# First mixer pair prepared among the last projection units of a fused two-block kernel

## The chip, the cores and the metric

The kernel runs on one core of a Trainium2 chip. The metric is the device time of one execution in microseconds, lower is better. Three runs of the kernel before gave 3347.84, 3348.26 and 3350.40 us; their median, 3348.26, is the time before.

## The reference

Two transformer blocks over 1024 tokens of width 1024, in float32. The change lies in the first block, between its projection and its mixer:

```python
xn = rms_norm(h, ln_attn_pre); proj = xn @ w_in          # 26 tiles of 128 columns
xs = p + (token_shift(p) - p) * mu                       # the first 14 tiles only
r, k, v, w_lo, a_lo, g_lo = split(xs)
decay = exp(-DECAY_SCALE * sigmoid(w_decay0 + tanh(w_lo) @ w_decay_up))
a = sigmoid(w_iclr0 + a_lo @ w_iclr_up);  g = sigmoid(g_lo) @ w_gate_up
kk = (k * k_k);  kk = kk / max(norm(kk per head), 1e-12)
k = k * (1 + (a - 1) * k_a)
state = state * w_t + (state @ -kk_t) (kk_t * a_t) + v_t k_t ;  y_t = state @ r_t
...
q, k, v of 4 differential heads -> softmax(q1 k1) - lam * softmax(q2 k2), times v
mix = concat(y_rwkv, attention);  h = h + rms_norm(mix @ w_out)
```

After it come the feed-forward part, and a second block with its own attention and feed-forward part, which the change does not touch.

## The kernel before

**Precision.** A matrix product in the projections is three products of high and low halves (`xh`, `xl`, `wh`, `wl`). One *unit* is one tile of 128 output columns: 48 matmuls of 128x512 (8 k-tiles, 3 parts, 2 halves of the tokens). ScalarE splits off the high half of a weight tile (`split_hi`), GpSimd the low half (`split_lo`), SP loads it (`load_w`).

**The order of the first block.** Units 0 to 11 of `ORDER1` (the tiles of q, k and v of the differential attention) run first, undisturbed. Then comes the *attention stream* (`d1_program_*`): four heads b, each with eight query blocks n. For each (b, n) TensorE computes the scores of block n+2 (`scores`), turns the probabilities of block n (`turn`), and multiplies them with the values (`output`). VectorE takes maxima with the bias (`maxima`), row-sum inverses (`inverse`), combines the two softmaxes (`combine`) and copies the output out of the bank (`output`, tile `osb`); ScalarE exponentiates and scales. In steps n=1 to 3 of head b the output of head b-1 is normed (`normed`), turned (`turn_output`), and split into `ost` by ScalarE and `ost_lo` by VectorE (`low`). These orders are written out by hand for each engine, and the names in `d1_names` must follow them.

Among these small products lie *fills*, matmuls of the remaining 14 projection units (u = 0 to 13, tiles 12, 13, 0, 4, 8, 1, 5, 9, 2, 6, 10, 3, 7, 11: the low-rank inputs, then r, k and v of the mixer's four pairs). `FILL1[b][n]` says how many follow each turned group. All units use banks 6 and 7. VectorE takes a finished unit out of the banks (`evac`, 128x1024) and one step later mixes it with its shifted copy (`shift`, two operations), SP stores it to `proj1`. 24 fills (`TAIL1`) remain after the last head.

**The seam.** After the stream each engine but SP drains and waits for all (`phase_end`). ScalarE takes tanh and sigmoid of the reloaded low-rank inputs `wa` and `gl`; then the first pair of the mixer is *prepared*, in parts that every engine knows by name:

- `lora0`, `lora1`: TensorE, 2 small products per half; ScalarE, sigmoids into `sg` and `iclr`
- `ksq`, `norm`, `root`: ScalarE squares k; TensorE sums over a head with `headones`; ScalarE takes the root into `kb`
- `sum`, `clamp`, `rc0` to `rc3`, `keys`, `mixed`, `decayed`, `ends`: VectorE, a scan over each chunk, the clamped reciprocals, and the scaled r, k, kk into `ar`, `bt`, `ktl`; between them ScalarE's three exponentials (`decays`), and GpSimd's `Bh`, `Kh` and `z`

Then come the score products (`scores_of_block`, `scores_pe`), their masks on VectorE (`scores_dve`, `strict_scores_dve`) and the mixer's levels for pairs j = 0 to 3. The preparation of pairs 1 to 3 lies within the pair before. `rkv` (r, k, v of a pair) has its home in the place of `xh`, so it is loaded after the last unit.

Of the kernel before, what the change touches and what calls it, by code (L numbers as in the profile page):

```python
# [8 lines left out]
F32 = mybir.dt.float32  # L9
# [100 lines left out]
def build_program(nc, a, out):  # L110
    ctx = ExitStack()
    with ctx:
# [34 lines left out]
        diff_t = at("diff_t", 161, [P, T])  # L147
# [60 lines left out]
        rkv = at("rkv", 16, [P, 3, T])  # L208
        sg = at("sg", 156, [P, T])
# [37 lines left out]
        abias = at("abias", 128, [P, T])  # L247
        pt1 = at("pt1", 132, [P, 2, T])
        osb1 = [at("osb1_0", 140, [P, TT, P]), at("osb1_1", 200, [P, TT, P])]
        pbuf1 = at("pbuf1", 165, [P, 3, 2, T])  # L250
        ost1 = at("ost1", 189, [P, 2, HALF], F32R)
        ost1_lo = at("ost1_lo", 193, [P, 2, HALF], F32R)
        sq_out = at("sq_out", 197, [P, P])
        negmax1 = at("negmax1", 197.5, [P, TT, 2])
        rowsum1 = at("rowsum1", 197.625, [P, TT, 2])
        weight1 = at("weight1", 197.75, [P, TT])
        osq1 = at("osq1", 197.875, [P, TT])
# [47 lines left out]
        phase = sem("phase")  # L305
# [124 lines left out]
        def phase_end(eng, k):  # L430

            eng.drain().then_inc(phase, 1)
            eng.wait_ge(phase, 4 * k)


        lora_ready = sem("lora_ready")
        lora_w_ready = sem("lora_w_ready")
# [12 lines left out]
        pre_pe = Steps(sem("pre_pe"), ["d0", "i0", "d1", "i1", "n0", "n1"])  # L450
        pre_act = Steps(sem("pre_act"), ["w0", "a0", "w1", "a1", "ksq", "r0", "r1", "P", "Pi", "Pp"])
        pre_dve = Steps(sem("pre_dve"), ["css", "cp", "clamp", "rc0", "rc1", "rc2", "rc3", "kk", "kb", "ka", "km",
                                         "A", "R", "Bt", "Kt", "pc"])
        pre_pool = Steps(sem("pre_pool"), ["Bh", "Kh", "z"])
# [33 lines left out]
        def prepare_pe(pe, j, what, first=False):  # L488
            mm = nc.tensor.matmul
            if what == "lora0" or what == "lora1":  # L490
# [4 lines left out]
                if h == 0 and not first:  # L495
# [3 lines left out]
                pre_pe.done(mm(ps[:, 3, :], lora_w[0:64, :], wa[0:64, half], start=True, stop=True), f"d{h}")  # L499
                if h == 0 and not first:  # L500
# [3 lines left out]
                pre_pe.done(mm(ps[:, 7, :], lora_w[64:128, :], wa[64:128, half], start=True, stop=True), f"i{h}")  # L504
            else:
                pre_act.wait(pe, "ksq", j)
                if not first:
                    rw_act.wait(pe, "n41", j - 1)
                for h in range(2):
                    pre_pe.done(mm(ps[:, 2 + 4 * h, :], headones[:, :], kk[:, h * HALF:(h + 1) * HALF], start=True,  # L510
                                   stop=True), f"n{h}")

        def scores_of_block(pe, j, b):

            if b == 0:
                pre_dve.wait(pe, "Bt", j)
                rw_dve.wait(pe, "G1", j - 1)
# [155 lines left out]
        def rwkv_pe(pe, j):  # L673
            last = j == RWKV_TILES - 1
            first_level_pe(pe, j)
            turn_pe(pe, j, "tV0", rkv[:, 2, :])
            turn_pe(pe, j, "tV1", rkv[:, 2, :])
            level_pe(pe, j, 1, "N")
            rw_act.wait(pe, "tV0", j)
            pre_pool.wait(pe, "z", j)  # L680
            pe.wait_ge(rk_heads_ready, 1)
            for b in range(NBLK):
                ins = nc.tensor.matmul(ps[:, 3, 2 * b:2 * b + 2], rkv[:, 0, b * P:(b + 1) * P], rk_heads[:, j, :],
# [39 lines left out]
            else:  # L723
                pre_act.wait(pe, "r1", j + 1)
# [77 lines left out]
        def prepare_act(act, j, what):  # L802
            if what[:4] == "lora":
# [4 lines left out]
                for k, n, to, bank, bias_ in (("d", "w", sg, 3, "w_decay0"), ("i", "a", iclr, 7, "w_iclr0")):  # L808
                    pre_pe.wait(act, f"{k}{h}", j)
                    pre_act.done(fn_act(to[:, half], ps[:, bank, :], ACT.Sigmoid, bias=col(bias_, j)), f"{n}{h}")  # L810
            elif what == "ksq":
                act.wait_ge(rkv_ready, 48 * j + 48)
                pre_dve.wait(act, "Bt", j - 1)
                pre_act.done(fn_act(kk[:, :], rkv[:, 1, :], ACT.Square, scale=col("k_k", j)), "ksq")
            elif what == "root":
                for h in range(2):
                    pre_pe.wait(act, f"n{h}", j)
                    pre_act.done(fn_act(kb[:, h * HALF:(h + 1) * HALF], ps[:, 2 + 4 * h, :], ACT.Sqrt), f"r{h}")
            else:
# [124 lines left out]
        def prepare_dve(dve, j, what):  # L944
            tt, stt = nc.vector.tensor_tensor, nc.vector.scalar_tensor_tensor
            done = pre_dve.done
            k = rkv[:, 1, :]
            if what == "sum":
                pre_act.wait(dve, "w1", j)
                pre_act.wait(dve, "Pi", j - 1)  # L950
                done(nc.vector.tensor_tensor_scan(css[:, :], chunk_mask[:, :], sg[:, :], 0.0, ALU.mult, ALU.add), "css")
                pre_dve.wait(dve, "css", j)
                done(tt(sg[:, :], css[:, :], sg[:, :], ALU.subtract), "cp")
            elif what == "clamp":
                pre_act.wait(dve, "r1", j)
# [5 lines left out]
            elif what == "keys":  # L961
                pre_dve.wait(dve, "rc3", j)
                pre_pe.wait(dve, "n1", j)
# [9 lines left out]
            elif what == "decayed":  # L973
# [5 lines left out]
                done(tt(ar[:, :, 1, :], blocks(rkv[:, 0, :]), blocks(dec[:, :]), ALU.mult), "R")  # L979
# [145 lines left out]
        def prepare_pool(pool, j):  # L1125
# [7 lines left out]
            pre_pool.done(tt(rkv[:, 0, :], rkv[:, 0, :], rkv[:, 1, :], ALU.mult), "z")  # L1133
# [40 lines left out]
        FOUR1 = [[16], [16], [16], [16], [16, 16], [16, 32], [12, 12], [12, 12]]  # L1174
        LEAD1, TAIL1 = [12, 12], [24]
# [1884 lines left out]
```

## Time and profile before

| | |
|---|---|
| median of three runs | 3348.26 us |
| the profiled execution | 3346.37 us, its span 3344.7 us |
| granted TensorE clock, mean | 0.972 |
| TensorE busy | 3078.1 us, 92% of the span |
| VectorE, ScalarE, GpSimd busy | 1586.2, 971.2, 678.0 us |
| stream, from its first fill to its last output | about 178.4 to 444.5 us |
| seam, last output to first mixer scores | 444.5 to 495.7 us |

Times in the trace are microseconds from the start of the span. A row of an engine gives start, length, engine, line, operation and the tiles it writes and reads; what stands in brackets is the idle time of the engine just before it, and what ended it. Matmul records overlap by their pipeline depth, so the distance between starts is the time that one costs.

### The profile page before, as it was taken

The numbers are of one execution on the slowest core, as the hardware profiler recorded it, in microseconds if no ns is written. First come the engines' busy times: TensorE is split into PE (matmuls) and PEld (weight loads), VectorE is DVE, ScalarE is ACT, GpSimd is POOL, SyncE is SP. The second block draws the span as 40 slices with busy tenths as digits, with TensorE's granted clock in tenths as the row PEclk, the third lists the DMA queues.
The fourth block names the chain that finished last, engine by engine and source line by source line (L and its number), as shares of the span: only waits on it lengthen the run. The fifth ranks groups of instructions, "written<-read, shape, count | busy, mean of one in ns | idle before, by whom it ended". The sixth has DMA issues, their size and how long they took to land.

```text
span 3344.7 us, 48677 instructions
## 1 busy us (share of the span) xinstructions
PE 3078.1 (92%) x20334; PEld 2467.4 (74%) x20334; DVE 1586.2 (47%) x1898; ACT 971.2 (29%) x1434; POOL 678.0 (20%) x292
## 2 busy tenths in 40 slices
PE   7999958889699999999699999999799999999998
PEld 5877747777488788887568876666588877778776
DVE  3155556851644444444551125455544554444545
ACT  3154435542322212221231123333432311111112
POOL 2311112222422112121153410000022212222220
PEclk9999979999899999999899999999999999999999
DMA  4443321012311111111053624335444311111111
GB/s 171 149 122 101 101 84 42 25 36 82 125 58 44 50 38 52 48 44 44 17 176 125 194 73 150 124 109 155 159 158 132 121 50 50 50 50 50 44 33 62
DMA packets 233976, 292.69 MB, mean 88 GB/s; under 512 B 10057, under 2 KB 182226, under 8 KB 233818
## 3 DMA queue, kind: packets, MB, share of 16 engines
q1 hardware_dynamic: 218842, 243.22, 23.8%
q10 hardware_dynamic: 14976, 47.19, 3.6%
q8 instruction: 120, 1.97, 0.2%
q14 instruction: 38, 0.31, 0.0%
HBM read 209.86 MB, written 80.51 MB: 87 GB/s over the span
## 4 chain that ended last, share of the span: by engine, by line
PE 82%; DVE 8%; issue 5%; ACT 3%; DMA 1%; POOL 1%; SPq 0%; DVEq 0%; ACTq 0%; POOLq 0%
PE ps L358 57%; PE ps L1797 5%; PE ps L1288 4%; PE ps L484 4%; PE ps L1867 2%; PE ps L1848 2%; DVE cb L2374 1%; PE ps L1351 1%; PE ps L1825 1%; DVE y L2284 1%; PE ps L1828 1%; POOL src L2177 1%; DVE xl L399 1%; PE ps L1311 1%; PE ps L1329 1%
## 5 line engine op out<-in xcount | busy, mean ns | idle before, releaser
L335 POOL TENSOR_TENSOR wl<-wraw,wh 128x1024 fp32r<-128x1024 f32 x151 | 368.6, 2441 | 1655.9 <-ACT wh L330 1655.9
L358 PE MATMUL ps<-xh,wh 128*128 128x512 f32 x2192 | 685.5, 394 | 7.0 <-POOL xl L1138 2.0
L358 PE MATMUL ps<-xl,wh 128*128 128x512 f32 x2192 | 676.8, 390 | 0.0
L358 PE MATMUL ps<-xh,wl 128*128 128x512 f32 x2192 | 676.0, 390 | 0.0
L358 PEld LDWEIGHTS ps<-xh,wh 128*128 128x128 f32 x2192 | 411.6, 188 | 104.1 <-issue 7.4
L358 PEld LDWEIGHTS ps<-xl,wh 128*128 128x128 f32 x2192 | 413.1, 188 | 86.4
L358 PEld LDWEIGHTS ps<-xh,wl 128*128 128x128 f32 x2192 | 412.3, 188 | 86.1
L330 ACT ACTIVATE wh<-wraw 128x1024 fp32r<-128x1024 f32 x167 | 177.0, 1060 | 971.9 <-PE ps L358 886.9
L2284 DVE TENSOR_TENSOR y<-ps,y 128x1024 f32<-128x1024 f32 x208 | 252.4, 1223 | 254.3 <-PE ps L358 254.3
L2205 POOL TENSOR_TENSOR dl<-draw,dh 128x2048 fp32r<-128x2048 f32 x27 | 128.0, 4739 | 611.4 <-ACT dh L2201 611.4
L358 PE MATMUL ps<-dh,fh 128*128 128x512 f32 x512 | 160.7, 395 | 21.3 <-DVE y L2284 15.5
L2323 DVE SCALAR_TENSOR_TENSOR cb<-ub,cols,cb 128x1024 f32<-128x1024 f32 x88 | 128.4, 1459 | 80.2 <-ACT cb L2351 74.2
L358 PE MATMUL ps<-dl,fh 128*128 128x512 f32 x512 | 158.8, 391 | 0.0
L358 PE MATMUL ps<-dh,fl 128*128 128x512 f32 x512 | 158.6, 391 | 0.0
L358 PE MATMUL ps<-fh,dh 128*128 128x512 f32 x352 | 113.2, 404 | 29.0 <-DVE y L2284 19.1
L2317 DVE TENSOR_TENSOR ub<-ps,rstd 128x1024 f32<-128x1024 f32 x44 | 53.9, 1225 | 178.2 <-PE ps L358 178.1
L1989 DVE CUSTOM_DVE_ANT_0 pbuf<-ps,bias 128x640 f32<-128x640 f32 (+7 forms) x128 | 85.6, 705 | 102.5 <-PE ps L1833 58.9
L358 PEld LDWEIGHTS ps<-dh,fh 128*128 128x128 f32 x512 | 95.7, 189 | 46.4 <-DVE y L2284 21.0
L2371 DVE TENSOR_TENSOR cb<-ps,rstd 128x1024 f32<-128x1024 f32 x32 | 39.2, 1224 | 183.0 <-PE ps L358 182.8
L2201 ACT ACTIVATE dh<-draw 128x2048 fp32r<-128x2048 f32 x27 | 51.6, 1912 | 252.1 <-PE ps L358 252.1
L358 PEld LDWEIGHTS ps<-dl,fh 128*128 128x128 f32 x512 | 96.8, 189 | 20.6
L358 PE MATMUL ps<-fl,dh 128*128 128x512 f32 x352 | 112.0, 400 | 0.0
(310 smaller groups left out, 4473.5 us busy)
## 6 DMA issues: line engine op xcount, KB each, us to landing
wraw<-in_w_up SPq DMA_DIRECT2D x76, 512.0 KB, 4.0
wraw<-in_w_in SPq DMA_DIRECT2D x67, 512.0 KB, 4.2
draw<-in_w_down SPq DMA_DIRECT2D x27, 1024.0 KB, 5.0
residual<-src ACTq DMA_DIRECT2D x32, 512.0 KB, 4.8
proj<-stage SPq DMA_DIRECT2D x30, 512.0 KB, 3.0
qk_hi<-hs ACTq DMA_DIRECT2D x24, 512.0 KB, 2.8
qk_lo<-ls SPq DMA_DIRECT2D x24, 512.0 KB, 2.9
kh<-qk_hi SPq DMA_DIRECT2D x48, 256.0 KB, 6.9
```

What stands on the lines that cost most here:

```text
L330: nc.scalar.activation(wh[:, s, :, :], wraw[:, s, :, :], ACT.Copy).then_inc(w_hi, 1)
L335: nc.gpsimd.tensor_tensor(wl[:, s, :, :], wraw[:, s, :, :], wh[:, s, :, :].bitcast(F32), ALU.subtract).then_inc(w_lo, 1)
L358: mm = nc.tensor.matmul(ps[:, bank + h, :], w, x[:, h * HALF:(h + 1) * HALF], start=start and k == 0, stop=stop and k == 2)
L484: return nc.tensor.matmul(to, left, right, **kw)
L1288: ins = mm(ps[:, 6 + h, :], w[:, s, kt, :], x[:, kt, h * HALF:(h + 1) * HALF], start=kt == 0 and part == 0, stop=kt == KT - 1 and part == 2)
L1797: ins = mm(ps[:, 6 + h, :], w[:, s, kt, :], x[:, kt, h * HALF:(h + 1) * HALF], start=kt == 0 and part == 0, stop=kt == KT - 1 and part == 2)
L1848: ins = nc.tensor.transpose(ps[:, bank, (k - 4 * g) * P:(k - 4 * g + 1) * P], pbuf[:, (TT * b + n) % 3, m, k * P:(k + 1) * P], ident[:, :])
L1867: ins = mm(ps[ROWS[m], 5, at_ + lo:at_ + hi], vt2[b % 2][:, kb, ROWS[m]], pt2[:, pair % 2, kb, m, lo:hi], start=kb == old[0], stop=True, s ...
L1989: a2_dve.done(nc.vector.tensor_tensor_reduce(pbuf[:, step % 3, m, 0:size], ps[:, 2 * m:2 * m + 2, :].rearrange("p a n -> p (a n)")[:, 0:size],
L2205: nc.gpsimd.tensor_tensor(dl[:, :, :], draw[:, :, :], dh[:, :, :].bitcast(F32), ALU.subtract)\
L2284: nc.vector.tensor_tensor(y[:, m, :], bank2(2 + m % 2), y[:, m, :], ALU.add).then_inc(down_added, 1)
L2323: ff1_dve.done(nc.vector.scalar_tensor_tensor(out=cb[:, r, :], in0=ub[:, r, 2 - back:T + 2 - back], scalar=col_at("conv_w", (2 - back) * 2 ...
```

## The change

- The last three units (u = 11, 12, 13, the tiles of pair 3) follow the last head: 144 fills in seven pieces (`TAIL1`). The 120 that are new there leave heads 1 and 2: groups of 16 become 9 in steps n=0 to 3, and 16 and 32 become 12 in n=4 and 5.
- Between the pieces stand the turns of the last head's output and the first pair's `norm`, `lora0` and `lora1` on TensorE; the other engines have its parts among the evacuations and splits of the three units.
- Unit 12 uses banks 2 and 3, norm banks 4 and 5, lora banks 0 and 1.
- `phase_end` is gone. The first pair's r, k and v have homes of their own (`rkv0`), z is written to `kk`; `stage1`, `diff_t` and the stream's tiles move in SBUF so that nothing is shared. The step counters are split (`pre_norm`, `pre_root`, `pre_sum`, `pre_z`), since the first pair's order now differs.
- `ends` of the first pair comes after the strict masks, behind a wait for the last stores of `proj1`; so do GpSimd's `Bh` and `Kh`.
- SP loads `wa`, `gl` and r, k, v of pair 0 right after storing unit 10, the low-rank and gate weights ahead of the stream.
- In the stream `low` stands behind `output` in VectorE's order.

```diff
-        FOUR1 = [[16], [16], [16], [16], [16, 16], [16, 32], [12, 12], [12, 12]]
-        LEAD1, TAIL1 = [12, 12], [24]
-        FILL1 = [[[6], [6], [6], [6], *THREE1[4:]], FOUR1, FOUR1, [*THREE1[:6], [6, 6], [6, 6]]]
+        MIDDLE1 = [[9], [9], [9], [9], *THREE1[4:]]
+        LEAD1, TAIL1 = [12, 12], [24, 12, 12, 12, 12, 24, 48]
+        FILL1 = [[[6], [6], [6], [6], *THREE1[4:]], MIDDLE1, MIDDLE1, [*THREE1[:6], [6, 6], [6, 6]]]
...
 # TensorE, after the last head
+            b = HEADS1 - 1
             fill(TAIL1[0])
-            turn_output(HEADS1 - 1, 0)
-            turn_output(HEADS1 - 1, 1)
+            turn_output(b, 0)
+            fill(TAIL1[1])
+            turn_output(b, 1)
+            fill(TAIL1[2])
             bank_free([])
+            d1_dve.wait(pe, f"os{b}{TT - 1}", 0)
+            prepare_pe(pe, 0, "norm")
+            fill(TAIL1[3])
+            pe.wait_ge(lora_act, 1)
+            prepare_pe(pe, 0, "lora0")
+            fill(TAIL1[4])
+            prepare_pe(pe, 0, "lora1")
+            fill(TAIL1[5])
+            fill(TAIL1[6])
...
 # ScalarE
-            split_hi(act, IN_TILES + 1, 1)
             root(b)
+            act.wait_ge(lora_ready, 16)
+            nc.scalar.activation(wa[0:64, :], wa[0:64, :], ACT.Tanh).then_inc(lora_act, 1)
             output(b, 0)
             output(b, 1)
             store(b)
+            prepare_act(act, 0, "ksq")
+            split_hi(act, IN_TILES - 1, 1)
+            prepare_act(act, 0, "root")
+            prepare_act(act, 0, "lora0")
+            prepare_act(act, 0, "lora1")
+            act.wait_ge(gl_ready, 16)
+            nc.scalar.activation(gl[:, :], gl[:, :], ACT.Sigmoid).then_inc(lora_act, 1)
+            split_hi(act, IN_TILES, 0)
+            prepare_act(act, 0, "decays")
+            split_hi(act, IN_TILES + 1, 1)
...
 # VectorE, in the stream
-                    if n in (2, 3) and b:
-                        low(b - 1, n - 2)
                     if n:
                         output(b, n - 1)
+                    if n in (2, 3) and b:
+                        low(b - 1, n - 2)
...
 # VectorE, after the last head
             output(b, TT - 1)
             shift()
-            evac(13)
             normed(b)
-            shift()
             low(b, 0)
             low(b, 1)
+            evac(11)
+            shift()
+            for what in ("clamp", "rc0", "rc1", "rc2", "rc3", "sum"):
+                prepare_dve(dve, 0, what)
+            evac(12)
+            shift()
+            for what in ("keys", "mixed", "decayed"):
+                prepare_dve(dve, 0, what)
+            evac(13)
+            shift()
...
 # SP
+                    if b == HEADS1:
+                        sp.wait_ge(stage_stored[0], 16 * 5)
+                        sp.wait_ge(stage_stored[1], 16 * 4)
+                        d1_pe.wait(sp, f"s{b - 1}{TT - 1}", 0)
+                        sp.dma_start(wa[:, :], proj1[WA_TILE]).then_inc(lora_ready, 16)
+                        sp.dma_start(gl[:, :], proj1[G_TILE]).then_inc(gl_ready, 16)
+                        d1_pe.wait(sp, f"o{b - 1}{TT - 1}", 0)
+                        for k in (1, 0, 2):
+                            sp.dma_start(rkv0[k][:, :], proj1[RWKV_TILES * k]).then_inc(rkv_ready, 16)
...
 # GpSimd, prepare_pool
+            if j == 0:
+                pre_z.done(tt(kk[:, :], rkv_of(0, 0), rkv_of(0, 1), ALU.mult), "z")
+                for s in range(2):
+                    pool.wait_ge(stage_stored[s], STAGES1)
             pre_pool.done(tt(chunks(bhc), chunks(bt), ends, ALU.mult), "Bh")
...
 # VectorE, rwkv_dve
+            if j == 0:
+                dve.wait_ge(stage_ready, SHIFTED_TILES)
             strict_scores_dve(dve, j)
+            if j == 0:
+                for s in range(2):
+                    dve.wait_ge(stage_stored[s], STAGES1)
+                prepare_dve(dve, 0, "ends")
...
 # between stream and mixer
-            phase_end(dve, 1)
-            dve.wait_ge(parked1_stored, 32 * HEADS1)
-            for what in ("sum", "clamp", "rc0", "rc1", "rc2", "rc3", "keys", "mixed", "decayed"):
-                prepare_dve(dve, 0, what)
             scores_dve(dve, 0)
-            prepare_dve(dve, 0, "ends")
```

## Rows read from the trace of the kernel before

**Rows 1.** The page, chain that ended last, by engine.

```profile
PE 82%; DVE 8%; issue 5%; ACT 3%; DMA 1%; POOL 1%; SPq 0%; DVEq 0%; ACTq 0%; POOLq 0%
```

**Rows 2.** The chain in order of time: start, length, what.

```profile
266.82 1.93 PE ps L1351 x8
268.75 1.49 PE ps L1311 x4
...
415.02 1.13 PE ps L1351 x8
416.15 0.81 PE ps L1311 x4
...
444.71 5.49 PE ps L1288 x24
```

**Rows 3.** Timeline of TensorE at the seam.

```profile
468.45 1.21 PE L499 MATMUL ps<-wa,lora_w 64*128 64x512 f32 x1 [8.89 <-ACTq L432]
...
475.83 3.78 PE L510 MATMUL ps<-kk,headones 128*128 128x512 f32 x4 [1.82 <-ACT kk L814]
495.68 3.60 PE L484 MATMUL ps<-ar,bt 64*64 64x128 f32 x64 [16.07 <-DVE bt L981]
...
502.52 1.15 PE L484 MATMUL ps<-mm_sb,mm_n 64*64 64x64 f32 x32 [1.29 <-DVE mm_n L1002]
```

**Rows 4.** Windows: TensorE, weights, VectorE, ScalarE, GpSimd busy; clock; DMA.

```profile
480.00:490.00 10.00, 0.00 (x0) 0.00 (x0) 9.62 (x7) 4.48 (x5) 0.00 (x0) 0.50 0.00 0
```

**Rows 5.** Timeline of VectorE at the seam.

```profile
450.23 1.23 DVE L1532 TENSOR_TENSOR shifted<-ps,rstd 128x1024 f32<-128x1024 f32 x1 [5.18 <-PE ps L1288]
...
456.38 1.28 DVE L1545 SCALAR_TENSOR_TENSOR stage<-diff_t,cols,shifted 128x1024 f32<-128x1024 f32 x1
...
474.37 2.29 DVE L951 TENSOR_TENSOR_SCAN css<-chunk_mask,sg 128x1024 f32<-128x1024 f32 x1 [13.30 <-ACT sg L810]
...
481.01 6.59 DVE L960 RECIPROCAL kb<-kb 128x256 f32<-128x256 f32 x4
...
494.41 1.22 DVE L981 TENSOR_TENSOR bt<-kb,dec_inv 128x1024 f32<-128x1024 f32 x1
...
501.78 1.28 DVE L1002 TENSOR_TENSOR mm_n<-ps,strict_t 128x512 f32<-128x512 f32 x2
```

**Rows 6.** DMA issues, 440 to 475 us: KB each, us to landing.

```profile
rkv<-proj SPq DMA_DIRECT2D x3, 512.0 KB, 8.8
...
wa<-proj SPq DMA_DIRECT2D x1, 512.0 KB, 5.4
```

**Rows 7.** Windows of heads 1 and 3, columns as in rows 4.

```profile
240.00:314.70 74.70, 69.12 (x364) 56.10 (x364) 45.64 (x94) 34.49 (x76) 10.03 (x4) 0.98 0.39 114
...
389.40:444.50 55.10, 50.65 (x277) 40.56 (x277) 36.23 (x76) 29.21 (x64) 4.81 (x2) 0.97 0.20 68
```

**Rows 8.** Timeline of TensorE in heads 1 and 3.

```profile
258.13 0.91 PE L1351 MATMUL ps<-vt,pt 128*128 128x128 f32 x6 [1.85 <-DVE osb L1512]
...
271.27 0.70 PE L1288 MATMUL ps<-xh,wl 128*128 128x512 f32 x2
...
398.39 0.68 PE L1351 MATMUL ps<-vt,pt 128*128 128x128 f32 x4 [0.70 <-DVE osb L1512]
...
405.75 0.91 PE L1351 MATMUL ps<-vt,pt 128*128 128x128 f32 x6 [1.85 <-DVE osb L1512]
...
417.90 0.70 PE L1288 MATMUL ps<-xh,wh 128*128 128x512 f32 x2
```

**Rows 9.** Timeline of VectorE in head 3.

```profile
394.71 1.66 DVE L1520 TENSOR_SCALAR osb<-osb,osq 128x128 f32<-128x128 f32 x8
...
404.65 0.75 DVE L1524 SCALAR_TENSOR_TENSOR ost_lo<-ps,small,ost 128x512 fp32r<-128x512 f32 x1 [2.65 <-ACT ost L1421]
405.32 0.28 DVE L1512 COPY osb<-ps 128x128 f32<-128x128 f32 x1
```

**Rows 10.** Timeline of ScalarE at the seam, last of three exponentials.

```profile
483.47 1.04 ACT L826 ACTIVATE sg<-sg 128x1024 f32<-128x1024 f32 x1
```

More of the change, by code:

```diff
@@ L484, in tile64, with rkv_of, lora_bank, norm_bank @@
             return nc.tensor.matmul(to, left, right, **kw)
-        def prepare_pe(pe, j, what, first=False):
+        def rkv_of(j, k):
+            return rkv[:, k, :] if j else rkv0[k][:, :]
+        def lora_bank(j, k):
+            return 3 + 4 * k if j else k
+        def norm_bank(j, h):
+            return 2 + 4 * h if j else 4 + h
+        def prepare_pe(pe, j, what):
             mm = nc.tensor.matmul
@@ L494, in prepare_pe @@
                     pe.wait_ge(lora_w_ready, 32 * j + 32)
-                if h == 0 and not first:
+                if h == 0 and j:
                     rw_act.wait(pe, "bonus", j - 1)
@@ L498, in prepare_pe @@
                     pre_act.wait(pe, "w0", j)
-                pre_pe.done(mm(ps[:, 3, :], lora_w[0:64, :], wa[0:64, half], start=True, stop=True), f"d{h}")
-                if h == 0 and not first:
+                pre_pe.done(mm(ps[:, lora_bank(j, 0), :], lora_w[0:64, :], wa[0:64, half], start=True, stop=True), f"d{h}")
+                if h == 0 and j:
                     rw_act.wait(pe, "tV1", j - 1)
@@ L854, in turned_act @@
                 rw_pe.wait(act, f"t{k}{h}", j)
+                if k == "V" and j == 0:
+                    pre_z.wait(act, "z", 0)
                 if k == "V" and h == 0:
@@ L2436, in rwkv_loads @@
             def rwkv_loads(j):
-                pre_dve.wait(sp, "Kt", j - 1)
-                rw_pe.wait(sp, "bonus", j - 1)
+                if j >= 2:
+                    pre_dve.wait(sp, "Kt", j - 1)
+                    rw_pe.wait(sp, "bonus", j - 1)
                 for k in range(3):
@@ L2566, in _ @@
         def _(pool):
-            for steps in (pre_pool, rw_pool, out_pool):
+            for steps in (pre_pool, pre_z, rw_pool, out_pool):
                 steps.start(pool)
@@ L2706, in _ @@
                 else:
-                    act.dma_start(proj1[ORDER1[u]], stage[:, s, :]).then_inc(stage_stored[s], 16)
+                    act.dma_start(proj1[ORDER1[u]], stage1[:, s, :]).then_inc(stage_stored[s], 16)
             d1_program_act(act)
-            act.wait_ge(lora_ready, 32)
-            nc.scalar.activation(wa[0:64, :], wa[0:64, :], ACT.Tanh).then_inc(lora_act, 1)
-            nc.scalar.activation(gl[:, :], gl[:, :], ACT.Sigmoid).then_inc(lora_act, 1)
-            for s in range(2):
-                act.wait_ge(stage_stored[s], STAGES1)
-            phase_end(act, 1)
-            for what in ("lora0", "lora1", "ksq", "root", "decays"):
-                prepare_act(act, 0, what)
+            act.wait_ge(parked1_stored, 32 * HEADS1)
             for j in range(RWKV_TILES):
@@ L2788, in _ @@
         def _(pe):
-            for steps in (pre_pe, sc_pe, rw_pe, out_pe, d1_pe, a2_pe):
+            for steps in (pre_pe, pre_norm, sc_pe, rw_pe, out_pe, d1_pe, a2_pe):
                 steps.start(pe)
@@ L2813, in _ @@
             d1_program_pe(pe)
-            phase_end(pe, 1)
             pe.wait_ge(lora_act, 2)
-            for what in ("lora0", "lora1", "norm"):
-                prepare_pe(pe, 0, what, first=True)
             for b in range(NBLK):
```

140 lines of the change are left out of this document (74 added, 66 removed).

## The prediction

> **What bounds the kernel now.** I read the page's chain of waits first: TensorE carries 82% of it and no other engine 10% [rows 1]. So a change is worth what it takes out of TensorE's waiting, and I looked for the place where TensorE waits longest. That is the seam between the attention stream and the mixer. The chain has the last fill, 24 matmuls in 5.49 us from 444.71 [rows 2]; that is 0.229 us for one. Then nothing of size runs until the first scores at 495.68, after 16.07 us of idle before them, and the first level starts at 502.52 [rows 3]. In between the granted clock is 0.50, the lower level of 1.2 GHz [rows 4]. From the stream's end (444.5) to the scores is 51.2 us, to the first level 58.0.
>
> The seam is a serial chain. VectorE waits 13.30 us, then does scan, reciprocals, keys and decays until bt at 494.41 + 1.22 [rows 5]. Ahead of it stand reloads of data that had long been in memory (5.4 us for wa, 8.8 for rkv [rows 6]) and the barrier, whose 8.89 us wait stands at the lora matmuls [rows 3].
>
> Then I read the stream by heads. Heads 1 and 2 (192 fills each) take 74.70 us, with TensorE busy 69; head 3 (120 fills) takes 55.10, busy 50.65 [rows 7]. The difference, 19.6, is 72 fills (16.5) and some 3 us of value turns and scores for a next head, which head 3 lacks. So the heads are TensorE-bound but for a few waits. Of these two of 1.85 us stand in each of heads 1 to 3, before `output` at n=2 and 3, put down to osb [rows 8]. VectorE shows why: `low` (ost_lo, 404.65) waits for ScalarE and holds the 0.28 us copy behind it (405.32), which frees `output` at 405.75 [rows 8, 9].
>
> **The change, part by part.**
>
> *Fills moved.* 60 of 192 fills leave heads 1 and 2 each: 28 in steps n=0 to 3, 32 in n=4 and 5. Each is 0.229 us [rows 2]: 6.4 and 7.3 us a head, 27.5 in all, which TensorE makes up in the tail. In n=4 and 5 head 3 shows that 12 to a group still cover the chain (its n=4 fill starts at 417.90 and the tail's at 444.7: 26.8 us; head 1's part from 271.27 to 314.77, less 56 fills (12.8) and 4.2 us for the next head, gives 26.5). There all 7.3 us return. In n=0 to 3 they don't:
> - `output` of n=1 waits for osb behind `normed`, which itself waits for the root on ScalarE. In head 3 that wait was 0.70, ending 398.39, 8.95 us after the head's start [rows 8]; VectorE's `normed` from 394.71 sets it [rows 9], and fewer fills don't move it. With 18 fills before it instead of the 24 of head 3, the wait grows by 1.4 to 2.1. That eats 2.1 of the 6.4 in heads 1 and 2; head 3 keeps its 0.7.
> - A shift of 2.5 us (two operations, the second 1.28 [rows 5]) now falls in n=2 of heads 2 and 3, since units 5 and 8 end in n=1. VectorE then reaches osb for `output` of n=3 only some 2.1 us late with 9 fills and 1.5 with 12. Head 1 has none there, 0.3.
>
> *`low` behind the copy.* The two waits of 1.85 go [rows 8]; what is late next is `combine`, still behind `low`, while TensorE has `output` and the next scores (0.91 + 1.4) as cover. 0.2 of each stays: 3.3 us a head back, 9.9 in all.
>
> *The clock in the stream.* After those waits it fell once in each of the three heads: 8 outputs took 1.93 instead of 1.13 and the scores 1.49 instead of 0.81 [rows 2]: 1.5 us each, 4.5 in all. The new waits of about 2 us have the same size, so I count two falls of three as gone: 3.0; bounds 0 and 4.5.
>
> The TensorE page of the Trainium skill ("TensorE: Matmul & The Clock Gate", Part 1: The HAM clock gate) says that the clock is throttled by default and only recent activity releases it. That speaks against the change where it opens new waits; by it all three falls could stay, and the sum would be 3.0 smaller. The three falls above agree with it.
>
> Sum of the stream: heads 1, 2 and 3 give 13.7 - 2.1 - 0.3 = 11.3, 13.7 - 2.1 - 2.1 = 9.5 and -1.5, plus 9.9 for `low` and 3.0 for the clock: 32.2 us. As a check I worked wait by wait to the start of the n=4 fills, which before is 31.2 us into heads 1 and 2 and 28.5 into head 3 [rows 7, 8]: after the change 21.9, 23.8 and 24.4. With 7.3 for the later steps of heads 1 and 2 that gives 35.4 without a clock fall, 33.9 with one, 32.4 with two. I take 32, bounds 29 and 35.5.
>
> *The tail*, counted from the stream's end. TensorE has 144 fills (33.0), two turns (1.2), norm (3.78 at the half clock [rows 3], so 1.9), and two lora halves (a pair 1.21 at half clock [rows 3]; some 1.1 a half at full, bound 2.1). That is 38.3 of work.
> - Turn 1 waits for ot0 and lo0. ScalarE puts tanh before ot0, and tanh waits for wa, issued once SP has stored unit 10, about 3.6. In the crowd at the seam wa took 5.4 [rows 6]; there are no parked stores beside it, so I take 4 (bounds 3 and 6). Tanh ends 8.6, ot0 9.3, lo0 10.1, TensorE ready at 8.9: wait 1.3. Unit 11 ends 13.5.
> - Norm waits for ksq, behind all three mixer loads. Issued by 6.2, they land by 13.5 by the 8.8 of [rows 6] less the parked stores. Wait 1.3.
> - The rest of TensorE finds its inputs: unit 12 ends 29.8, unit 13 40.8. The splits of units 13 and 26 are on ScalarE and GpSimd with over 8 us to spare.
> - VectorE: evac and shift of unit 11 until 17.3 (1.23 + 2.5 [rows 5]); root, clamp, reciprocals (6.59) 25.5; sum (scan 2.29, and 1.22 as bt) 29.1; evac and shift of unit 12 33.6; keys to bt, 8.0 as from 487.6 to 495.6, 41.6. ScalarE's three exponentials (last one 483.47, 1.04 [rows 10]) wait for unit 12's split and end by 35.2, hidden. Evac 13 ends 42.95, and the scores wait for it: 43.1 instead of 51.2.
> - Then VectorE still has the shift (2.5) before the score masks, which need 4 x 0.65, and the strict ones 0.65 [rows 5]. The first level starts at 48.9 instead of 58.0: 9.1 us. Kt, Bh and Kh move behind the last stores' landing (about 48.6); I1 of GpSimd, which the products W1 wait for, then comes some 0.4 us later against the first level's start than before. TensorE has the first level, the value turns, N1, the bonus and M1 before W1, so that is hidden; without that cover it would cost its 0.4.
>
> A clock fall in the tail, after the two waits of 1.3, would cost 1.5; I keep it in the range.
>
> *At nothing:* the barrier and the wait for the parked stores (both in the seam already counted); the new wait for the residual store at unit 0, which ended before 57; later loads of pair 1, which go earlier; table loads, five before and after; tile homes. Each has cover of several us.
>
> Total: 32 + 9 = 41 us. The profiled execution takes 3346.37 (span 3344.7 and 1.7 around it), 1.9 below the median of 3348.26. 3346.4 - 41 = 3305.4, and against the median 3307.
>
> **Rivals.**
> 1. *The heads don't return their fills.* If VectorE and ScalarE bound steps n=0 to 3 of heads 1 and 2, all 12.8 us of those fills stay there as waits, instead of the 6.6 counted. For it: the osb wait. Against: `output` waits have other causes removed here. Loss 6 more, with the clock falls 3 more: 3316. Chance 0.16.
> 2. *The tail stretches.* TensorE is in order, and ksq, tanh, the roots and the evacuations queue on engines that wait for one another. If wa lands 2 us later and the loads 4 later, TensorE's finish and all behind it move by 5 to 8: 3314. For it: 8.8 for the loads. Against: those ran beside 1 MB of parked stores. Chance 0.18.
> 3. *Reordering frees nothing*, since `combine` behind `low` binds as much: 9.9 and part of the clock lost, 3318. Against: the next scores lie between. Chance 0.05.
> 4. *The other side: the clock stays at 1.2 GHz through the tail and into the mixer*, as it did from 460 to 490 [rows 4]. The tail's 38 us of work would take 38 more, so 3345. It decides for slower than before by 0.2% once another 10 us of the mixer's TensorE work also runs at that level: 3355 and more. Against: fills are dense where before there was nothing. Chance 0.02 for 3345, 0.02 for slower.
>
> **How the numbers follow.** The forecast of 3307 has 0.57, with its own range 3302 to 3312: 1.5 to 4.5 of clock, 2 of DMA landings, 2 of the new waits. The range's lower edge is 3299: a tail without its two waits (2.6) and the stream's upper bound (3.5) beyond it. The rivals 1 and 2 end by 3320. Range 3299 to 3320. A measurement tells 0.2% (6.7 us) from no change. Faster has 0.57 + 0.16 + 0.18 + 0.05 = 0.96, less 0.01 for mishaps; same 0.02; slower 0.03.
>
> **What would show it.** Heads 1, 2 and 3 of 58, 60 and 51 us, 1.5 more in one where the clock falls; no 1.85 wait on osb at n=2, but one of about 2 at n=1; first scores 43 us after the stream's last output; first level 49; TensorE's clock near 1.0 throughout; VectorE's evac 13 just after bt. The prediction is wrong if a tail wait on wa, ksq or a root exceeds 5 us, or if heads 1 and 2 stay above 66.

## The result, and the profile after

The changed kernel takes 3326.57 us (median of 6 runs, 3322.08 to 3333.68) against 3349.33 for the kernel before beside it (6 runs, 3343.24 to 3353.09): a ratio of 0.9936, 95% interval 0.9921 to 0.9951. It is faster, as forecast, by 23 us and not by 41; 3326.57 lies above the range of 3299 to 3320. The profiled execution has a span of 3326.1 us, against 3344.7.

I put the two traces side by side at three marks: the heads, the first projection fill behind the stream's last output (the tail begins), and the first level of the mixer's inverse. TensorE's timeline has the last two.

```profile
427.16 0.70 PE L1320 MATMUL ps<-xh,wh 128*128 128x512 f32 x2
...
478.76 3.69 PE L484 MATMUL ps<-ar,bt 64*64 64x128 f32 x64 [6.56 <-DVE shifted L1587]
485.43 1.15 PE L484 MATMUL ps<-mm_sb,mm_n 64*64 64x64 f32 x32 [0.52 <-DVE mm_n L1017]
```

The first level starts at 485.43 instead of 502.52 [rows 3]: 17.1 us of the span's 18.6. The windows (columns as in rows 4) are heads 1, 2, 3 and the tail:

```profile
240.67:309.86 69.19, 59.26 (x304) 47.10 (x305) 38.49 (x89) 32.04 (x74) 4.74 (x2) 0.93 0.37 107
309.86:376.31 66.45, 57.03 (x304) 45.55 (x305) 39.99 (x90) 33.23 (x75) 7.12 (x3) 0.95 0.38 111
376.31:427.16 50.85, 48.99 (x276) 39.48 (x277) 35.00 (x75) 29.99 (x65) 5.08 (x3) 1.00 0.19 63
427.16:485.43 58.27, 47.53 (x304) 36.76 (x302) 46.36 (x43) 22.16 (x27) 12.53 (x6) 0.88 0.33 118
```

The stream ends 17.3 us sooner (427.16 for 444.5) where 32 were forecast, and the tail takes 58.3 us, as long as the seam did before, where 48.9 were forecast. Head 3 came out as worked out (50.85 for 51). Heads 1 and 2 did not: 69.19 and 66.45 for 58 and 60. TensorE is idle in them for 9.9 and 9.4 us, and its clock is lower than before (0.93 and 0.95, 0.98 in [rows 7]). Heads 1 and 2 above 66 us were a sign of being wrong that the prediction had named, and it came. The waits of TensorE from 240 to 376 us name the cause (total, times, longest):

```profile
PE ps L1320 <- DVE shifted L1587: 10.9, 3, 4.9
PE ps L1383 <- DVE osb L1567: 4.1, 3, 2.1
PE ps L1343 <- DVE negmax L1548: 2.1, 2, 1.1
```

L1320 is the fill, L1587 is `evac`. In the kernel before, TensorE has no wait of this kind in heads 1 and 2. The osb waits, of which the forecast spoke, are there and are 4.1 us.

### The profile page after: what moved, and what is told of

The parts are those of the page before. It is cut to its first block, busy times and chain, and to the rows that moved or that the text cites. A ratio compares the mean times of both kernels' runs of the same rounds, so it can differ in the third digit from the quotient of the medians.

```text
span 3326.1 us, 48681 instructions
## 1 busy us (share of the span) xinstructions
PE 3082.3 (93%) x20334; PEld 2472.0 (74%) x20334; DVE 1592.1 (48%) x1898; ACT 969.9 (29%) x1434; POOL 677.0 (20%) x292
## 4 chain that ended last, share of the span: by engine, by line
PE 80%; DVE 10%; issue 5%; ACT 3%; DMA 1%; POOL 1%; SPq 0%; DVEq 0%; ACTq 0%; POOLq 0%
PE ps L359 58%; PE ps L1870 5%; PE ps L484 4%; PE ps L1320 3%; PE ps L1940 2%; PE ps L1921 2%; DVE cb L2447 1%; DVE xl L400 1%; PE ps L1898 1%; PE ps L1383 1%; DVE y L2357 1%; PE ps L1901 1%; POOL src L2250 1%; DMA vraw<-proj 1%; DVE cb L2396 1%
## 5 line engine op out<-in xcount | busy, mean ns | idle before, releaser
L359 PEld LDWEIGHTS ps<-dh,fl 128*128 128x128 f32 x512 | 96.7, 189 | 20.4
```

The source lines that it names most:

```text
L359: mm = nc.tensor.matmul(ps[:, bank + h, :], w, x[:, h * HALF:(h + 1) * HALF], start=start and k == 0, stop=stop and k == 2)
```

## Experiments

Ten runs, each with the kernel before timed on the same chip. An eleventh, e8 (the changed kernel with 32 of the 1024 columns of the first pair's reciprocals computed), has no time, and e11 put its question again. The marks of each, from its profiled execution (us; heads 1, 2 and 3; the tail up to the first level; the time of the first level, and the rest of the span behind it):

| kernel | median | ratio, 95% interval | heads | tail | first level | rest |
|---|---|---|---|---|---|---|
| before | 3349.33 | | 74.7, 74.7, 55.0 | 58.0 | 502.5 | 2842.2 |
| changed | 3326.57 | 0.9936 [0.9921, 0.9951] | 69.2, 66.5, 50.9 | 58.3 | 485.4 | 2840.7 |
| e1 | 3332.65 | 0.9958 [0.9941, 0.9976] | 70.3, 70.3, 50.7 | 58.1 | 490.9 | 2836.6 |
| e5 | 3352.45 | 1.0008 [0.9995, 1.0022] | 64.7, 59.2, 54.8 | 88.7 | 508.4 | 2842.4 |
| e2 | 3307.06 | 0.9877 [0.9861, 0.9894] | 60.4, 54.8, 50.9 | 55.8 | 461.9 | 2839.9 |
| e3 | 3329.87 | 0.9940 [0.9922, 0.9958] | | 59.5 | 487.2 | 2846.2 |
| e4 | 3321.96 | 0.9922 [0.9900, 0.9944] | | 52.1 | 478.3 | 2839.8 |
| e6 | 3300.61 | 0.9855 [0.9832, 0.9879] | 60.4, 55.2, 50.9 | 54.0 | 461.4 | 2838.2 |
| e9 (e6 again) | 3310.66 | 0.9883 [0.9864, 0.9901] | | 52.4 | 459.6 | 2843.8 |
| e7 | 3305.18 | 0.9870 [0.9846, 0.9893] | | 49.4 | 455.3 | 2837.7 |
| e10 (e7 again) | 3299.06 | 0.9844 [0.9827, 0.9860] | | 49.4 | 455.6 | 2851.6 |
| e11 | 3300.91 (one run) | | | 47.9 | 455.2 | 2844.0 |

The last column matters for reading the rest. Behind the first level all these kernels do nearly the same work (e11 on other values; the first pair's `ends`, `Bh` and `Kh`, and from e4 on two of GpSimd's splits, lie on one side of the mark or the other), and it takes between 2836.6 and 2851.6 us. e7 and e10 are one program, and differ there by 14 us. The windows of that stretch, e7 first (columns as in rows 4):

```profile
455.34:3293.00 2837.66, 2648.83 (x18152) 2127.91 (x18152) 1351.94 (x1481) 776.49 (x1077) 584.72 (x229) 0.98 0.26 82
```

```profile
455.56:3307.20 2851.64, 2662.31 (x18153) 2137.99 (x18152) 1352.55 (x1481) 776.98 (x1077) 584.69 (x229) 0.97 0.26 81
```

TensorE's busy time makes 13.5 of the 14.0 us, at a lower mean clock, with the same matmuls and the other engines unchanged. Up to the first level the two agree within 0.3 us, so marks there separate kernels that medians of a few runs do not. They are not free of chance either: e6 and e9, one program too, differ there by 1.8 us.

**e1: the kernel before, with only `low` moved behind `output`.**

```diff
+                    if n:
+                        output(b, n - 1)
                     if n in (2, 3) and b:
                         low(b - 1, n - 2)
-                    if n:
-                        output(b, n - 1)
```

(the same exchange in the list of VectorE's steps)

> The kernel before with only VectorE's ost_lo moved behind its osb copy. Theory (the prediction's term): the six waits of 1.85 us before output at n=2 and 3 of heads 1 to 3 shrink to 0.2 to 0.3, heads 1 and 2 take 71.4 us or 1.5 less where the clock fall goes, and the whole is 10 to 14 us faster. Rival: the wait moves to combine, which still stands behind ost_lo: turn waits instead, and the whole is 0 to 3 us faster.

The heads lose 4.4, 4.3 and 4.3 us, 13.1 in all, where the forecast had 9.9 + 3.0, and the clock is 1.00 in all three. Two windows of 70 us, as long as the heads (columns as in rows 4):

```profile
240.00:310.00 70.00, 67.14 (x365) 54.59 (x363) 45.38 (x91) 34.09 (x75) 9.89 (x4) 1.00 0.41 121
310.00:380.00 70.00, 67.14 (x363) 54.47 (x363) 45.46 (x92) 34.23 (x75) 9.69 (x5) 1.00 0.41 121
```

Where the kernel before waited 1.85 us at `output` of n=2 and 3 [rows 8], nothing waits. At the first level 11.6 us of the 13.1 are there, since head 1 starts 1.4 us later; that is most of the change's 17.1 from this one exchange.

**e5: the kernel before, with only the fills moved.** 48 fills leave head 1 and 72 leave head 2, and all 144 stand in one block ahead of the barrier, beside none of the mixer's preparation. The counts are such that each unit ends with a step, which those of the change (60 and 60) are not.

```diff
...
-        LEAD1, TAIL1 = [12, 12], [24]
-        FILL1 = [[[6], [6], [6], [6], *THREE1[4:]], FOUR1, FOUR1, [*THREE1[:6], [6, 6], [6, 6]]]
+        LEAD1, TAIL1 = [12, 12], [144]
+        FILL1 = [[[6], [6], [6], [6], *THREE1[4:]], THREE1, [*THREE1[:6], [6, 6], [6, 6]], [*THREE1[:6], [6, 6], [6, 6]]]
```

> The kernel before with only the fills moved: 120 from heads 1 and 2 (counts that end units with steps) behind the last head, as one block of 144 ahead of the barrier; preparation, order of ost_lo and homes as before. Theory: the fills leave the heads at 0.23 us each, 27 us, less about 1.5 us of new waits, and come back in the block, so the time is within 3 us of before; the gain of the whole change then comes from what covers them. Rival: the emptier heads don't give the fills back, and the kernel is 6 us or more slower.

Heads 1 and 2 fall to 64.7 and 59.2 us. That is 25.5 us for 120 fills, at 0.229 us each 27.5, so heads whose units end with steps return nearly all. The tail takes it back and more (88.7 for 58.0): the first level is 5.9 us later than before, between the theory's 3 and the rival's 6, and the time can't be told from that of before (0.9995 to 1.0022). Moving the fills gains nothing by itself. What it can gain is the cover that they give the preparation, less what the heads keep.

**e2: the changed kernel, with other counts of fills, so that each unit ends with a step.**

```diff
-        MIDDLE1 = [[9], [9], [9], [9], *THREE1[4:]]
-        FILL1 = [[[6], [6], [6], [6], *THREE1[4:]], MIDDLE1, MIDDLE1, [*THREE1[:6], [6, 6], [6, 6]]]
+        FILL1 = [[[6], [6], [6], [6], *THREE1[4:]], THREE1, [*THREE1[:6], [6, 6], [6, 6]], [*THREE1[:6], [6, 6], [6, 6]]]
```

> The changed kernel with the same number of fills in the stream and in the tail, but 12 to a group in head 1 and head 3's counts in head 2, so that every unit ends with a step. Theory: the three waits of a next unit's first fill for the evacuation (2.74, 3.27 and 4.86 us, 10.9 in all) go; about 2 us of them come back as osb waits, and clock falls in heads 1 and 2 go with them, so heads 1 and 2 together take 9 to 15 us less than their 135.6. Rival: VectorE is the bound of the emptier heads, and the waits return elsewhere; the two heads take at most 3 us less.

```profile
PE ps L1342 <- DVE negmax L1547: 3.2, 3, 1.1
PE ps L1382 <- DVE osb L1566: 1.4, 2, 0.7
PE ps L1319 <- DVE shifted L1586: 1.1, 2, 0.6
```

```profile
240.15:300.52 60.37, 56.82 (x316) 45.72 (x316) 40.14 (x90) 32.96 (x75) 7.65 (x3) 1.00 0.41 123
300.52:355.29 54.77, 51.58 (x292) 41.14 (x292) 38.82 (x89) 32.02 (x74) 4.80 (x2) 1.00 0.45 135
...
406.14:461.90 55.76, 44.11 (x304) 33.69 (x302) 47.03 (x43) 22.26 (x27) 13.40 (x6) 0.94 0.34 123
```

(First TensorE's waits from 240 to 356 us, then the windows of heads 1 and 2 and of the tail.) Heads 1 and 2 together hold as many matmuls as before the edit (608) and take 20.5 us less: the waits on `evac` fall from 10.9 to 1.1 (0.6 each), those on osb from 4.1 to 1.4, and the clock is 1.00. Of the 20.5, 12.6 are idle time of TensorE and 7.9 are the same matmuls at the full clock (busy 108.4 for 116.3). That is more than the 9 to 15 expected. The edit also puts 12 fills and not 9 in steps n=0 to 3, which cover VectorE longer; the fall of the osb waits can come from that, and no run parts it from where the units end. The stream now ends at 406.14, 38 us sooner than before.

**e3: the changed kernel, with tanh behind the last value turns.** ScalarE's wait for wa stood ahead of `output` and held it.

```diff
-            act.wait_ge(lora_ready, 16)
-            nc.scalar.activation(wa[0:64, :], wa[0:64, :], ACT.Tanh).then_inc(lora_act, 1)
             output(b, 0)
             output(b, 1)
             store(b)
+            act.wait_ge(lora_ready, 16)
+            nc.scalar.activation(wa[0:64, :], wa[0:64, :], ACT.Tanh).then_inc(lora_act, 1)
```

> The changed kernel with tanh of wa (and its wait for the load) behind the last head's output on ScalarE. Theory: the 3.03 us wait before the second turn in the tail goes and the clock stays up there, unit 11 ends 6 us earlier; then norm waits for the loads of r, k and v until about 16.5 us into the tail, and the first level comes 2 to 5 us earlier. Rival: VectorE's chain sets the end of the tail whatever starts it; first level within 1 us of where it was.

The second turn no longer waits, and VectorE takes out unit 11 13.0 us into the tail instead of 19.0, the 6 us of the theory. But TensorE then meets the next late input, at the norm, behind the landing of r, k and v, and the clock falls there (3.75 us for 4 matmuls):

```profile
434.08 0.66 PE L1369 MATMUL ps<-ident,osb 128*128 128x128 f32 x4 [0.63 <-DVE osb L1575]
445.30 3.75 PE L519 MATMUL ps<-kk,headones 128*128 128x512 f32 x4 [4.59 <-ACT kk L827]
```

The tail is 59.5 us, no shorter than 58.3, near the rival's "within 1 us", but not for its reason. VectorE's chain is not full. It waits 1.42 us for unit 12's fills, whose evacuation starts 35.5 us into the tail in both kernels. TensorE's wait moved and set it there. The 1.2 us more come behind it, from a `diff_t` beside a whole split (3.42 us for 2.19):

```profile
463.23 1.23 DVE L1587 TENSOR_TENSOR shifted<-ps,rstd 128x1024 f32<-128x1024 f32 x1 [1.42 <-PE ps L1320]
464.50 3.42 DVE L1597 TENSOR_TENSOR diff_t<-shifted 128x1024 f32<-128x1024 f32 x1
```

**e4: the changed kernel, with GpSimd's weight splits kept away from VectorE's work.** The split for unit 13 runs only once unit 11 is staged (`stage_ready` 12), two further ones behind the bonus.

```diff
-            for n in range(2, IN_TILES + 2):
+            for n in range(2, IN_TILES):
+                if n == IN_TILES - 1:
+                    pool.wait_ge(stage_ready, 12)
                 split_lo(pool, n, n % 2)
...
+            if j == 0:
+                split_lo(pool, IN_TILES, 0)
+                split_lo(pool, IN_TILES + 1, 1)
```

> The changed kernel with GpSimd's split of unit 13 held until VectorE has mixed unit 11, and the two splits of the output projection's first weights moved behind the bonus product of the first pair. Theory: a VectorE operation with two tiles of SBUF as inputs stands still while GpSimd works; then diff_t of unit 11 takes 1.22 instead of 3.41, that of unit 12 1.22 instead of 2.19, bt 1.22 instead of 3.36, and the first level comes 5 us earlier. Rival: the long operations have another cause (TensorE at full rate, DMA); their lengths stay and the time is the same.

In VectorE's timeline the three slow operations are back at their usual length:

```profile
443.14 1.23 DVE L1600 TENSOR_TENSOR diff_t<-shifted 128x1024 f32<-128x1024 f32 x1
...
459.90 1.23 DVE L1600 TENSOR_TENSOR diff_t<-shifted 128x1024 f32<-128x1024 f32 x1
...
469.14 1.22 DVE L996 TENSOR_TENSOR bt<-kb,dec_inv 128x1024 f32<-128x1024 f32 x1
```

The tail falls from 58.3 to 52.1 us, 6.2 where the theory had 5. Only part of it is the splits':

```profile
438.46 0.63 PE L1372 MATMUL ps<-ident,osb 128*128 128x128 f32 x4 [2.48 <-DVE ost_lo L1582]
```

```profile
441.88 1.23 DVE L1590 TENSOR_TENSOR shifted<-ps,rstd 128x1024 f32<-128x1024 f32 x1 [1.28 <-PE ps L1323]
446.02 2.69 DVE L971 TENSOR_SCALAR kb<-kb 128x1024 f32<-128x1024 f32 x1 [0.33 <-ACT kb L831]
```

Unit 11's evacuation (441.88) starts 15.7 us into the tail instead of 19.0, before any moved split runs. wa landed after 4.7 us and not 5.3, the second turn waited 2.48 us, and the clock did not fall behind it. That is 3.3 of the 6.2. From there to the first level 2.9 are left: the three operations give 5.3, and the clamp, which now stands beside the moved split, takes 2.0 back, the wait ahead of it 0.3. The median is 4.6 lower, and the two intervals overlap, so this one rests on the marks.

**e6: e2 and e4 together.**

> The changed kernel with both earlier edits: units that end with steps, and GpSimd's splits out of VectorE's way. Theory: the two causes add: stream end near 406 as with the first, 52 us from there to the first level as with the second, so the first level near 458 and the kernel 26 us faster than the changed one, about 3301. Rival: they overlap, because both lower the tail's clock falls; first level at 461 or later.

The first level starts at 461.4, in the second execution (e9) at 459.6, against 461.9 in e2. The splits set aside give 1.8 and 3.4 us of tail, and not 6. The evacuation of unit 11 parts the tail in two. First TensorE's and VectorE's rows there in e2, then in e6:

```profile
418.51 0.63 PE L1368 MATMUL ps<-ident,osb 128*128 128x128 f32 x4 [2.62 <-DVE ost_lo L1578]
421.92 1.23 DVE L1586 TENSOR_TENSOR shifted<-ps,rstd 128x1024 f32<-128x1024 f32 x1 [1.27 <-PE ps L1319]
```

```profile
420.38 1.09 PE L1371 MATMUL ps<-ident,osb 128*128 128x128 f32 x4 [3.20 <-DVE ost_lo L1581]
426.48 1.23 DVE L1589 TENSOR_TENSOR shifted<-ps,rstd 128x1024 f32<-128x1024 f32 x1 [3.49 <-PE ps L1322]
```

Behind it e2 takes 40.0 us to the first level, e6 and e9 34.9 each: 5.1 us, what the splits cost. Ahead of it e2 takes 15.8, e6 19.0 and e9 17.5, by when wa landed (4.9, 5.4 and 5.0 us) and by the clock, which did not fall behind the waits of 2.48 (e4) and 2.62 (e2) and fell behind those of 2.75 (e9), 3.03 (the change) and 3.20 (e6). So the rival's 461 came in one of two executions, by the load's landing; what the edits add to or take from that landing is not shown.

**e7: e6, with k loaded first and its square ahead of tanh.** The last head's output no longer stands behind wa's landing, and the square of k waits for k alone. All loads are issued behind the last output's matmuls.

```diff
+                        sp.dma_start(rkv0[1][:, :], proj1[RWKV_TILES]).then_inc(k0_ready, 16)
                         sp.dma_start(wa[:, :], proj1[WA_TILE]).then_inc(lora_ready, 16)
...
+            output(b, 0)
+            output(b, 1)
+            prepare_act(act, 0, "ksq")
+            store(b)
             act.wait_ge(lora_ready, 16)
             nc.scalar.activation(wa[0:64, :], wa[0:64, :], ACT.Tanh).then_inc(lora_act, 1)
-            output(b, 0)
-            output(b, 1)
-            store(b)
-            prepare_act(act, 0, "ksq")
```

> As the one before, and in the tail the load of k first and on a semaphore of its own, ksq right behind the last head's output on ScalarE, tanh behind it. Theory: with both waits (for tanh and for the loads of r and v) out of TensorE's way the second turn and norm wait under 1 us each, unit 11 ends 13 us into the tail, the first level comes at 48 to 49 us, which is what the prediction had. Rival: VectorE's chain is full from its first step, and the tail stays at 51 to 52.

The tail is 49.4 us, the one forecast for the change itself (48.9). One turn waits 0.65 us, and that is all of TensorE's waiting before the scores:

```profile
412.26 0.66 PE L1375 MATMUL ps<-ident,osb 128*128 128x128 f32 x4 [0.65 <-DVE osb L1581]
448.68 3.69 PE L485 MATMUL ps<-ar,bt 64*64 64x128 f32 x64 [3.65 <-DVE shifted L1593]
```

Unit 11's evacuation starts 13.0 us into the tail, in e10 too. Behind it the kernel takes 36.4 us, 1.5 more than e6, since VectorE waits 1.02 for the root and the clamp stands beside the moved split (1.99 us for 0.69).

**e9 and e10: e6 and e7 again, on one chip in more rounds.**

> This is the kernel with units that end with steps and the splits set aside, once more and on the same chip as the next, in more rounds: its first median was 3300.6 us in 4 runs. If that median is its own, this one falls within 3 us of it, and the tail is 53 to 55 us with a wait of about 3 at the second value turn. If it was luck of the draw, it comes out above 3304.

> This is the kernel with the keys' load and square first, once more beside the kernel above. Its first four runs went from 3294.8 to 3309.4, its profiled tail was 49.4 us against 53.9. Theory, that the tail's 4.5 us are real: the median falls 3 to 5 us below that of the kernel above, near 3297. Rival, that the earlier loads cost elsewhere what they give here, or that the one profiled execution was a favourable one: the two medians lie within 2 us of each other.

E9's median came out 10 us above e6's, so the low first median was luck; e10's came out 6 below e7's. By the first medians alone e6 (3300.61) had looked faster than e7 (3305.18). The tails are 52.4 us (54.0 in e6) and 49.4 (49.4), the first levels 4.1 us apart. The medians' 11.6 are more than these marks explain; the profiled execution of e10 had 3308.97 us, the slowest of its five, by the stretch behind the first level. Taken together, nine runs of e7's kernel have a median of 3300.7 and eight of e6's 3305.8. Side by side in this last comparison the intervals, 0.9844 [0.9827, 0.9860] and 0.9883 [0.9864, 0.9901], do not touch; in the first they overlapped, and the nine and eight runs come from two chips. E7's kernel is the version to keep, some 50 us faster than before and 25 faster than the change.

**e11: e7 without the first pair's four reciprocals.** Its clamp also caps at 0.001, and four operations of 8 columns stand for the reciprocals, so the mixer's first pair works on other values.

> The kernel above, but the first pair's four reciprocals (6.59 us on VectorE) are left out: its clamp also caps at 0.001 and four operations of 8 columns stand in their place. VectorE works without a gap from unit 11's evacuation to the scores there. Theory: TensorE's units and the written order bind almost as tightly, since VectorE only reaches unit 12's evacuation at 435.7 where TensorE is through with the unit at about 434.0; so the scores start 1.6 us sooner, 3.7 us less before the first level at most, and 45 to 48 us of tail is left. Rival: VectorE's sum of work is the bound, and all of some 6 us comes back: a tail of 43.4 us.

```profile
435.55 1.23 DVE L1599 TENSOR_TENSOR shifted<-ps,rstd 128x1024 f32<-128x1024 f32 x1 [1.42 <-PE ps L1332]
```

```profile
448.55 2.77 PE L485 MATMUL ps<-ar,bt 64*64 64x128 f32 x64 [2.16 <-DVE shifted L1599]
```

The tail is 47.9, 1.5 us less: some 6 us less work on VectorE gave 1.5, for VectorE now waits 3.05 us for the sigmoids ahead of the scan and 1.42 for unit 12's fills. The theory held and the rival (43.4) fell. In e7 VectorE and TensorE are through with unit 12 within 1.5 us of each other, and a shorter tail needs both shorter, or another order.

## Why the prediction was right or wrong

*`low` behind the copy and the clock in the stream:* right. E1 alone gives 13.1 us in the heads for the 12.9 forecast. Head 3 took 50.7 us there and 50.85 in the changed kernel, for 51; the 1.5 us that the sum charged to it for later osb copies did not come.

*Fills moved:* wrong, and the larger miss (14.7 us in the stream; the tail missed by 9.4). The step that failed is "There all 7.3 us return", with the account of n=0 to 3 beside it: I counted the fills by steps and the new waits by osb and shift, and did not ask at which point of a step a unit of 48 fills now ends. A unit's first fill writes the banks that `evac` must have emptied, and VectorE comes to `evac` at the end of a step. Before, each unit ended with a step. With groups of 9 (16 before, 12 in e2) three units end inside one, at n=4 and 6 of head 1 and n=1 of head 2, and the next unit starts in the same step. The rows of TensorE and VectorE at the second such place:

```profile
288.37 0.49 PE L1361 MATMUL ps<-ident,pbuf 128*128 128x128 f32 x3
292.13 0.63 PE L1320 MATMUL ps<-xh,wh 128*128 128x512 f32 x1 [3.27 <-DVE shifted L1587]
```

```profile
288.90 0.56 DVE L1627 COPY pt<-ps 128x384 f32<-128x384 f32 x1 [3.25 <-PE ps L1361]
289.37 0.28 DVE L1567 COPY osb<-ps 128x128 f32<-128x128 f32 x1
289.57 1.28 DVE L1562 SCALAR_TENSOR_TENSOR pbuf<-pbuf,weight 128x1024 f32<-128x1024 f32 x1
290.76 1.22 DVE L1587 TENSOR_TENSOR shifted<-ps,rstd 128x1024 f32<-128x1024 f32 x1
```

TensorE has nothing from 288.86 to 292.13, since `evac` stands behind the step's last transposed copy and the next weighting. Three such waits took 2.74, 3.27 and 4.86 us, and the clock fell behind them. E2 ends the units with steps; the waits on `evac` all but went, and 20.5 us with them, more than the whole miss (its fuller steps n=0 to 3 have a part in it that is not known). So the forecast of 32 for the stream was itself 6 us low for counts that fit: e2's stream ends 38.4 us sooner, with fewer osb waits than I charged and no fall of the clock. The heads of 58, 60 and 51 us in the prediction were already nearer: they come from the count wait by wait, save 35.5 us, and were not brought in line with the 32.

*The tail:* wrong by 9.4 us. Of these 5.5 came up to unit 11's evacuation (19.0 us into the tail for 13.5) and 3.9 behind it. Three of its terms were short.

The second turn waited 3.03 us and not 1.3. I took 4 us for wa and said bounds of 3 and 6; it took 5.3 among five loads issued within 2.3 us. The last column is us to landing:

```profile
wa<-proj SPq DMA_DIRECT2D x1, 512.0 KB, 5.3
gl<-proj SPq DMA_DIRECT2D x1, 512.0 KB, 6.1
k<-proj SPq DMA_DIRECT2D x1, 512.0 KB, 6.5
```

```profile
437.38 1.06 ACT L1511 ACTIVATE wa<-wa 64x1024 f32<-64x1024 f32 x1 [6.29 <-DMA wa<-proj]
```

The clock fell behind this wait, which I had kept in the range and not in the sum: the 12 fills up to unit 11's end took 5.07 us in the chain of waits, 2.75 at the full clock. Unit 11 was done 19 us into the tail, not 13.5; the wait of 1.3 us that I had at the norm did not come.

The third term was not in the forecast: VectorE's operations stood still beside GpSimd's. VectorE first, then GpSimd:

```profile
447.39 3.41 DVE L1597 TENSOR_TENSOR diff_t<-shifted 128x1024 f32<-128x1024 f32 x1
...
462.66 1.22 DVE L1587 TENSOR_TENSOR shifted<-ps,rstd 128x1024 f32<-128x1024 f32 x1
463.92 2.19 DVE L1597 TENSOR_TENSOR diff_t<-shifted 128x1024 f32<-128x1024 f32 x1
...
474.12 3.36 DVE L996 TENSOR_TENSOR bt<-kb,dec_inv 128x1024 f32<-128x1024 f32 x1
477.40 1.21 DVE L1587 TENSOR_TENSOR shifted<-ps,rstd 128x1024 f32<-128x1024 f32 x1
```

```profile
447.32 2.39 POOL L336 TENSOR_TENSOR wl<-wraw,wh 128x1024 fp32r<-128x1024 f32 x1 [18.08 <-ACT wh L331]
462.56 2.46 POOL L336 TENSOR_TENSOR wl<-wraw,wh 128x1024 fp32r<-128x1024 f32 x1 [12.85 <-ACT wh L331]
473.43 2.97 POOL L336 TENSOR_TENSOR wl<-wraw,wh 128x1024 fp32r<-128x1024 f32 x1 [8.41 <-ACT wh L331]
```

Each slow operation ends some 1.1 us after GpSimd's (450.80 after 449.71, 466.11 after 465.02, 477.48 after 476.40), which is its usual 1.22: it did nothing until GpSimd was through. The evacuation at 462.66, which reads one operand from PSUM, kept its 1.22 beside the same split. The Trainium skill has the rule ("GPSIMD Engine Reference", Specifications): GpSimd shares its SBUF interfaces with VectorE, in contention with VectorE's instructions that have two SBUF inputs. The trace agrees. The three operations took 5.3 us more than their usual length, and e6 beside e2 shows 5.1 us behind unit 11's evacuation without them. I costed the splits as "with over 8 us to spare", by when their result is needed, and not by what runs beside them. The trace of before had the sign: a weighting of one element a partition that took 2.27 us while a split ran.

```profile
434.20 2.27 DVE L1501 TENSOR_TENSOR weight<-rowsum,small 128x1 f32<-128x1 f32 x1
```

These add to the forecast chain in order: VectorE, 99% busy from 450 to 485, reached unit 13's evacuation at 477.40, when TensorE had been waiting for over 5 us. The rest of VectorE's work up to there was 2.3 us shorter than I had counted, and from the scores to the first level it took 0.9 longer (6.7 for 5.8), with the scores at the half clock and unit 13's `diff_t` (2.41 us) beside GpSimd's product for z. With late inputs and splits out of the way (e7) unit 11's evacuation starts at 13.0 for 13.5, and behind it stand 36.4 us for 35.4: a tail of 49.4 for 48.9.

*The rivals.* The first (heads don't return their fills) and the second (the tail stretches) came both, which I had priced singly at 9 and at 5 to 8 us; they cost 14.7 and 9.4. Both were named from the right place with the wrong mechanism: not VectorE as the bound of the steps, but the place of `evac` in them; and not the loads alone. No common cause showed, and by my own prices both together come to 3324, which is above my range and near the 3326.57 measured. The loads' part of rival 2 held in kind: wa landed 1.3 us later than I took. Rival 3 and the clock staying at 1.2 GHz did not come; the clock was 0.88 in the tail.

*The forecast's 3307* is e2's time to the microsecond, but by two misses that cancel: its stream is 6 us shorter than forecast, and its tail 7 longer.

What stays open: what lowers TensorE's mean clock behind the first level in one execution and not in another (14 us between e7 and e10; all kernels lie within 15). And the scores run at the half clock (3.69 us) after a wait of even 3.65, and in 1.98 to 3.02 us after one of 2.16 (e6, e11, e9); no run tried to close it.

## What to carry to other kernels

When work is taken out of a stream that is written out by hand, follow not only how much is left in each step but where each accumulation now ends, and put that end where the engine that evacuates it has its turn: here, with fuller steps beside it, this was worth nearly as much as the whole change (20.5 and 23 us). Price an operation of GpSimd by what VectorE runs in that time, not only by when its result is due. When two runs of a stage differ, split the stage at a mark between the causes: in e4 half of a gain that fitted the theory was a load that landed sooner. A wait removed from an in-order engine comes back at its next late input (e3) until the inputs are loaded in the order in which they are used (e7).

## What the runs showed of the hardware

VectorE's operations with two inputs in SBUF that began beside a running operation of GpSimd stood until it was done: 1.22 us became 2.19 to 3.42, and one of a single column took 2.27 for 0.16. Where VectorE's began first it kept its length and GpSimd's stretched: `ar` at 472.98 took 1.22 us in the changed kernel, and the split that began at 473.43 took 2.97 for 2.39. VectorE's clamp, an operation with one input, took 2.69 in e4 (0.69 in the changed kernel) where a split had begun before it, and 0.69 in e6 where the split began after; e6's reciprocals, with one input too, kept their 6.59 us beside that split. Five loads of 512 KB issued within 2.3 us landed after 5.3 to 8.2 us, and the store issued 0.4 us ahead of them after 3.0.
